# Experts of a gated MoE kernel: all eight chunks of gate and up split, the output copied by one engine, one signal per chunk of w_down

## The reference

```python
a = jnp.einsum('td,edf->tef', hf, w_gate[g])
b = jnp.einsum('td,edf->tef', hf, w_up[g])
act = (jax.nn.silu(a) * b) * cg[..., None]
y = y + jnp.einsum('tef,efd->td', act, w_down[g])
```

## Time and profile before

| | |
|---|---|
| Runs (us) | 947.41, 949.59, 951.21; median 949.59 |
| Profiled execution (us) | 948.92 |
| Its span, first to last instruction (us) | 946.9 |
| TensorE busy | 920.6 us, 97% |
| VectorE busy | 698.5 us, 74% |
| ScalarE busy | 442.0 us, 47% |
| GpSimd busy | 83.3 us, 9% |
| Moved by DMA | 170.13 MB, mean 180 GB/s |

### The profile page before, as it was taken

The page is one execution under the profiler, slowest core; times in us unless marked ns, Lnnn a source line. Parts: engine busy times, 40 slices in busy tenths (PEclk is TensorE's granted clock), DMA queues, the critical chain, the costliest instruction groups (busy, mean ns, idle before and its releaser), DMA issues.

```text
span 946.9 us, 13479 instructions
## 1 busy us (share of the span) xinstructions
PE 920.6 (97%) x5016; PEld 815.8 (86%) x5016; DVE 698.5 (74%) x951; ACT 442.0 (47%) x694; POOL 83.3 (9%) x109
## 2 busy tenths in 40 slices
PE   8999999999999999999999999999999999999984
PEld 7999999999999999999888888778777878787751
DVE  5648797777878877437721348798989898989847
ACT  6612221312111138822401324587878787878714
POOL 0000000010000000000000002322121212121100
PEclk9999999999999999999999999999999999999998
DMA  9020111111111211012511765599999999999559
GB/s 301 12 67 23 45 46 45 39 37 45 56 35 46 89 45 45 12 34 90 174 57 37 259 244 222 195 348 396 365 381 376 362 370 359 378 376 380 226 205 367
DMA packets 73801, 170.13 MB, mean 180 GB/s; under 512 B 10907, under 2 KB 48299, under 8 KB 60401
## 3 DMA queue, kind: packets, MB, share of 16 engines
q1 hardware_dynamic: 64529, 152.05, 44.8%
q0 software_dynamic: 9216, 17.32, 5.7%
HBM read 156.83 MB, written 22.47 MB: 189 GB/s over the span
## 4 chain that ended last, share of the span: by engine, by line
PE 90%; DVE 5%; ACT 3%; issue 1%; DMA 1%; SPq 0%; ACTq 0%; DVEq 0%
PE ps L1682 42%; PE ps L1963 16%; PE ps L1870 11%; PE ps L1941 10%; PE ps L1956 3%; PE ps L1919 2%; PE ps L1824 2%; PE ps L1705 1%; DVE x L1656 1%; PE ps L1992 1%; PE ps L1811 1%; DVE x L1642 1%; PE ps L1927 1%; DVE hT L1083 1%; DMA xs<-in_x_prompt 1%
## 5 line engine op out<-in xcount | busy, mean ns | idle before, releaser
L1682 PE MATMUL ps<-hT,w_hi 128*128 128x352 f32 x1344 | 329.5, 326 | 0.8 <-DVE hT L1083 0.8
L1682 PEld LDWEIGHTS ps<-hT,w_hi 128*128 128x128 f32 x1344 | 235.9, 189 | 2.0 <-DVE hT L1083 1.2
L1682 PE MATMUL ps<-hT,w_lo 128*128 128x352 f32 x672 | 218.3, 325 | 0.0
L1157 DVE SCALAR_TENSOR_TENSOR C<-V,w_dw,C 128x1086 f32<-128x1086 f32 x120 | 154.8, 1345 | 0.3
L1531 DVE TENSOR_TENSOR wgu_lo<-wgu,wgu_hi 128x1024 fp32r<-128x1024 f32 (+1 forms) x128 | 133.8, 1086 | 1.3 <-ACT wgu_hi L988 1.1
L1682 PEld LDWEIGHTS ps<-hT,w_lo 128*128 128x128 f32 x672 | 126.2, 188 | 0.0
L988 ACT ACTIVATE wgu_hi<-wgu 128x1024 fp32r<-128x1024 f32 x124 | 114.9, 956 | 6.5 <-PE ps L1963 5.3
L1963 PE MATMUL ps<-wgu_hi,XT_hi 128*128 128x512 f32 x224 | 100.0, 447 | 0.0
L1558 DVE TENSOR_TENSOR wdn_lo<-wdn,wdn_hi 128x1024 fp32r<-128x1024 f32 x62 | 73.2, 1223 | 27.3 <-ACT wdn_hi L1024 27.3
L1090 DVE TENSOR_TENSOR w_lo<-w_raw,w_hi 128x1024 fp32r<-128x1024 f32 (+1 forms) x44 | 45.2, 1028 | 64.2 <-ACT w_hi L791 64.2
L1870 PE MATMUL ps<-wo_hi,hT 128*128 128x512 f32 x288 | 91.6, 399 | 0.0
(11 more groups left out here) (258 smaller groups left out, 1491.7 us busy)
## 6 DMA issues: line engine op xcount, KB each, us to landing
wgu<-in_w_gate SPq DMA_DIRECT2D x32, 1024.0 KB, 9.1
wgu<-in_w_up SPq DMA_DIRECT2D x32, 1024.0 KB, 11.5
wdn<-in_w_down SPq DMA_DIRECT2D x32, 1024.0 KB, 13.4
w_raw<-in_w_in SPq DMA_DIRECT2D x28, 512.0 KB, 3.8
yy<-YK SPq DMA_DIRECT2D x8, 1024.0 KB, 11.7
xs<-in_x_prompt SPq DMA_DIRECT2D x8, 512.0 KB, 7.6
wo_raw<-in_w_out SPq DMA_DIRECT2D x8, 512.0 KB, 4.9
xr<-in_x_prompt SPq DMA_DIRECT2D x16, 256.0 KB, 2.7
```

Of the source, the lines that this page charges most:

```text
L1157: op = dve.scalar_tensor_tensor(out=C[:, g, :], in0=V[:, g, k:k + CWID], scalar=w_dw[:, g, k:k + 1], in1=C[:, g, :], op0=ALU.mult, op1=ALU ...
L1682: op = pe.matmul(ps[:, bank_of(m, c), 0:CH], a[s][:, k, :], r[:, k, c * CH:(c + 1) * CH], start=(k == 0 and q == 0), stop=(k == K - 1 and ...
```

## The change

`WHOLE` becomes 0, so all eight chunks of gate and up are split, in four pieces of two chunks, and the tile `XT`, its copy and its fp32 product are gone. Both halves of `Y` are copied by ScalarE, one after the other; VectorE only makes the index column, which no longer waits for the down product. ScalarE gives a signal for each of the two chunks of w_down, and VectorE waits for each by itself, where it waited for both.

```diff
--- before.py
+++ after.py
@@ -44,7 +44,7 @@
 PASSES = (T + CAP - 1) // CAP
 TOP = 2048.0
 WB = 4
-WHOLE = 1
+WHOLE = 0
 PIECES = [slice(c, min(c + 2, KD)) for c in range(WHOLE, KD, 2)]
 PAIRS = len(PIECES)
 AHEAD = 2
@@ -228,7 +228,6 @@
         wdn = [at(f"wdn{u}", [P, KF, D], F32, w_off[u] + 16384) for u in range(WB)]
         X = at("X", [P, 4, D], F32, r_h + 49152)
         Y = [at(f"Y{u}", [P, D], F32, o) for u, o in enumerate((r_uv + 24576, r_uv + 28672, r_s + 4352, r_wo))]
-        XT = at("XT", [P, WHOLE, P], F32, r_yp + 24576)
         XT_hi = at("XT_hi", [P, KD - WHOLE, P], F32R, r_yp + 24576 + WHOLE * P * 4)
         XT_lo = at("XT_lo", [P, KD - WHOLE, P], F32R, r_yp + 24576 + KD * P * 4)
         assert 24576 + (2 * KD - WHOLE) * P * 4 <= 32768
@@ -528,7 +527,7 @@
 
         BIAS, LN_G, LN_B, SCALE = 0, GR, 2 * GR, 3 * GR
 
-        PREP = 10
+        PREP = 9
         RANK_BANK = (7, 3)
         FIND_BANK, FIND_AGAIN = 2, 4
 
@@ -1004,7 +1003,6 @@
 
                 act.wait_ge(s_tx, it + 1)
                 wait(act, s_gp, it * PAIRS)
-                act.activation(XT[:, :, 0:CAP], ps[:, 0, :].rearrange("p (c t) -> p c t", c=4)[:, 0:WHOLE, 0:CAP], ACT.Copy)
                 act.activation(XT_hi[:, :, 0:CAP], split_chunks(), ACT.Copy).then_inc(s_xtA, 1)
 
             def at_hi(u, it):
@@ -1016,13 +1014,14 @@
 
                 act.wait_ge(s_down, it + 1)
                 wait(act, s_ys[u], 16 * uses)
-                act.activation(Y[u][0:CAP, 0:512], ps[0:CAP, 4 + 2 * (u % 2), :], ACT.Copy).then_inc(s_yA, 1)
+                for h in range(2):
+                    op = act.activation(Y[u][0:CAP, h * 512:(h + 1) * 512], ps[0:CAP, 4 + 2 * (u % 2) + h, :], ACT.Copy)
+                op.then_inc(s_yA, 1)
 
             def down_hi(p, i, u, halves):
                 act.wait_ge(s_wn[u], 16 * (p * (GE // WB) + i + 1))
                 for c in range(KF):
-                    op = act.activation(halves[c][:], wdn[u][:, c, :], ACT.Copy)
-                op.then_inc(s_dnhi, 1)
+                    act.activation(halves[c][:], wdn[u][:, c, :], ACT.Copy).then_inc(s_dnhi, 1)
 
             def step(p, i, u):
                 it = p * GE + i * WB + u
@@ -1545,16 +1544,14 @@
 
                 dve.tensor_copy(g_now[0:CAP, u:u + 1], column(g_idx, e)).then_inc(s_gc, 1)
 
-            def y_out(it, u, uses, e):
-                dve.wait_ge(s_down, it + 1)
+            def s_column(u, uses, e):
                 wait(dve, s_ys[u], 16 * uses)
 
-                dve.tensor_copy(s_now[0:CAP, u:u + 1], column(s_idx, e))
-                dve.tensor_copy(Y[u][0:CAP, 512:1024], ps[0:CAP, 5 + 2 * (u % 2), :]).then_inc(s_yD, 1)
+                dve.tensor_copy(s_now[0:CAP, u:u + 1], column(s_idx, e)).then_inc(s_yD, 1)
 
             def down_lo(it, u, halves):
-                dve.wait_ge(s_dnhi, it + 1)
                 for c in range(KF):
+                    dve.wait_ge(s_dnhi, it * KF + c + 1)
                     op = dve.tensor_tensor(wdn_lo[u][:, c, :], wdn[u][:, c, :], halves[c][:].bitcast(F32), ALU.subtract)
                 op.then_inc(s_dnlo, 1)
 
@@ -1575,7 +1572,7 @@
                     for j in range(AHEAD, PAIRS):
                         gate_lo(it + 1, nu, j)
                 if not (isinstance(i, int) and i == 0 and u == 0):
-                    y_out(it - 1, (u - 1) % WB, p * (GE // WB) + i + (u - 1) // WB, i * WB + u - 1)
+                    s_column((u - 1) % WB, p * (GE // WB) + i + (u - 1) // WB, i * WB + u - 1)
                 dve.wait_ge(s_athi, it + 1)
                 dve.tensor_tensor(AT_lo[:, :, 0:CAP], act_turned(u), AT_hi[:, :, 0:CAP].bitcast(F32),
                                   ALU.subtract).then_inc(s_act, 1)
@@ -1612,7 +1609,7 @@
                 prep(dve.tensor_scalar(rank[:], rank[:], -float(CAP), None, ALU.add))
                 if isinstance(p, int):
                     dve.wait_ge(s_cnt, 1)
-                for half in (XT[:], XT_hi[:].bitcast(F32), XT_lo[:].bitcast(F32)):
+                for half in (XT_hi[:].bitcast(F32), XT_lo[:].bitcast(F32)):
                     prep(dve.memset(half[:, :, CAP:P], 0.0))
                 if isinstance(p, int):
                     dve.wait_ge(s_h2st[0], 16 * ((TILES + 1) // 2))
@@ -1626,7 +1623,7 @@
                 for j in range(AHEAD):
                     gate_lo(p * GE + 1, 1, j)
                 groups(dve, step, p)
-                y_out(p * GE + GE - 1, WB - 1, (p + 1) * (GE // WB) - 1, GE - 1)
+                s_column(WB - 1, (p + 1) * (GE // WB) - 1, GE - 1)
 
             rounds(dve, one)
 
@@ -1931,7 +1928,6 @@
                 b = u % 2
                 pe.wait_ge(s_act, it + 1)
                 wait(pe, s_yA, it - 1)
-                wait(pe, s_yD, it - 1)
                 pe.wait_ge(s_dnlo, it + 1)
                 for h in range(2):
                     cols = slice(h * 512, (h + 1) * 512)
@@ -1952,8 +1948,6 @@
                 pe.wait_ge(s_xtA, it + 1)
                 wait(pe, s_act, it - 1)
                 pe.wait_ge(s_wl[u], 32 * (p * (GE // WB) + i + 1))
-                for c in range(WHOLE):
-                    pe.matmul(both, XT[:, c, :], wgu[u][:, :, c, :], start=(c == 0), stop=False)
                 pe.wait_ge(s_xtD, it + 1)
                 for j in range(PAIRS):
                     pe.wait_ge(s_gl, it * PAIRS + j + 1)
```

## The result

| | before | after |
|---|---|---|
| median of 12 runs (us) | 948.51 | 954.34 |
| lowest to highest | 946.75 to 951.21 | 952.87 to 955.87 |
| ratio, 95% interval | | 1.0064 [1.0054, 1.0074] |
| profiled execution, its span | 948.92, 946.9 | 955.87, 954.1 |

The change made the kernel slower by 0.64%, 6.1 us (the medians differ by 5.8). The forecast was 948.9, no difference that can be measured, with a range that ended at 952.5.

A forecast was written before the change was run, and what follows sets the result against it. TensorE was taken to set the pace, with loads having no spare time. Start +1.1, saving -5.4 and end +0.85 gave -3.45; late loads cut this to -0.7, so 948.9 us in terms of the median, range 944.5 to 952.5.

The forecast's parts named there:

- TensorE's own saving: In each loop step, three fp32r matmuls replace the fp32 chunk: 0.18 us saved, a step of 9.26, -5.4 us over 30 steps.
- ScalarE, VectorE and the signals at nothing: In each loop step, the added work of ScalarE and VectorE and the changed signals cost nothing, covered by TensorE's work.
- Rival 3: At each step's first matmul, XT_lo becomes the bound: +13.8 us, with start and end +15.8, or 965.4; chance 0.05.
- The start: In the first two steps, three more matmuls follow the wait for XT_lo: 0.7 to 1.4 us, taken as +1.1.
- The loads take back the rest: Late in the loop, loads landing no earlier leave 1.6 us of a 3.9 us lead; net with the end -0.7.
- the wait for loads that I expected after 830 us: Late in the loop, ScalarE's wgu_hi waits for a load, up to 3 us at a time, TensorE idle by less.
- The prediction's own sign of being wrong: In the loop, the prediction counts as wrong if loads stall it by more than its whole lead, taken as 3.9 us.
- The end: In the last step, AT_hi comes 0.50 us later and the last Y about 0.35 later, together +0.85.
- Rival 2: Over the whole loop, loads pin the pace and leave no lead: +0.85 to +2, about 951 us; chance 0.13.
- rival 1: Over the whole loop, loads keep pace and land earlier with their issue: -3.45, or 946.1 us; chance 0.2.

The follow-up runs named there:

- e2_copy_signals: Against the kernel before: ScalarE alone copies Y and each w_down chunk has its signal, the fp32 chunk stays; 949.55 us, ratio 1.0005.
- e3_keep_running: The changed kernel plus identity matmuls in TensorE's idle time before the first products of steps 0 and 1; 952.16 us, ratio 1.0029.
- c2_after_light_keep: The changed kernel with w_down loads of 8 columns instead of 1,024, plus identity matmuls before the first products of steps 0 and 1; 946.23 us, ratio 0.9972.
- e4_hi_first: The changed kernel with the first piece's four products that need only XT_hi run before the two that need XT_lo; 948.55 us, ratio 0.9996.
- c1_hi_first_end: e4_hi_first with, in the last step, AT_hi made before Y is copied and the last Y copied by ScalarE and VectorE; 947.99 us, ratio 0.9992.
- c3_split_hi_first: Against the kernel before: only the split of all eight chunks, with the product order of e4_hi_first; 948.78 us, ratio 1.0006.
- e1_split_only: Against the kernel before: only the split of all eight chunks, Y copied by both engines and one w_down signal as before; 953.12 us, ratio 1.0040.

## Why the prediction was wrong

**TensorE's own saving** was right. From one step's products to the next it is 9.25 and 9.28 us (they start at 641.91, 651.16 and 660.44), against the forecast 9.26.

**ScalarE, VectorE and the signals at nothing** was right. TensorE is busy throughout from 647.6 to 818.1, and e2_copy_signals pays for the end alone. Rival 3, XT_lo as the bound of each step, did not come.

**The start** is the step that failed. "The first fp32r matmul waits for the same XT_lo, and three more matmuls come behind it": the first half held in step 0, with 601.87 where I wrote about 601.6; in step 1 it was 612.16, for about 610.0. But I priced what comes behind it by 0.23 us a product, the price at the full clock, and bounded the whole at 1.4 us. Measured, the loss is 5.06 by the end of step 1. The fp32 chunk not only filled the time of XT_lo; by running then it kept TensorE's clock up. Without it 24 products took 7.34 and 7.35 us, not 5.56, which is 3.6 for two steps; e3_keep_running and c2_after_light_keep give 3.1 and 3.6 for it. The remaining 1.5 is the wait of steps 0 and 1 and the three added products; e3_keep_running, at the full clock, has 1.95 for it. My upper bound of 1.4 was little under that. It is the fall of the clock that was priced at nothing: I took a TensorE that waits for a TensorE that costs only its wait. Nothing in the trace of before shows a clock below 1.00 in this stretch. But it has a price of this kind at the end of the loop, which I did not read. There TensorE is idle for 2.03 us; the granted clock is 0.73 from 908 to 910 and 0.50 from 910 to 912, and eight products take 5.40 us that take 3.43 soon after (chain of waits):

```profile
906.03 2.03 issue
908.05 5.40 PE ps L1992 x8
...
916.47 3.43 PE ps L1992 x8
```

The Trainium skill, in "TensorE: Matmul & The Clock Gate", section "What's actually happening", says that TensorE's default state is throttled and that activity releases it. These traces agree: 0.51 after 2.22 us of idle time in the changed kernel, 1.00 once e3_keep_running fills it.

**The loads take back the rest** was right as a mechanism and too small in size. I let the landings move back by at most the 1.1 us of the start. The start was late by 5.06, the first two up weights issued within the loop left 2.6 and 5.1 us later, and the landing of the weight issued near 796 moved back by 9.9. The rates account for most of that: by 647.6 the loads are behind by 40 GB/s x 47.6 us, 1.9 MB or 5.1 us at 376 GB/s; the 6 GB/s less in the next two stretches of 56.8 and 56.9 us add 1.8. The other 3.0 I can't place. So the wait for loads that I expected after 830 us, "with TensorE idle by less", came at 825.7, and TensorE's wait there cost 2.27 - 1.25 = 1.0 us at first and 5.65 - 2.27 = 3.4 in the next step, of which 7.32 - 5.56 = 1.8 is the third fall of the clock. The prediction's own sign of being wrong, loads that stall the loop by more than its whole lead, came true: TensorE was stalled by 4.4 us, and it had no lead but was 1.25 late.

**The end** was right in its two terms: AT_hi 0.47 later after Y (forecast 0.50), the last scatter 0.33 later after the last Y's start (0.35). But behind the last scatter, where the forecast put nothing, this execution lost another 2.05 us, and that stays open.

**The rivals.** Rival 2, loads that pin the loop at about 951, was nearest in time. With the start at its right price it gives 948.9 + (5.06 - 1.1) + 1.6 = 954.5, where 1.6 is the lead that the forecast still left to TensorE; the median is 954.34. That they agree so closely is luck: the sum starts from 949.59, the median of three runs, where that of twelve is 948.51, and it leaves out the 2.05 us behind the last scatter. Nor was the whole loop pinned: up to 815 TensorE made up 3.8 us, and only then did the loads hold it. With the cover back (e4_hi_first, c1_hi_first_end) the time is where the forecast had it, at no difference from before, and rival 1, loads that keep pace, is excluded by their waits of 13.1 and 14.7 us.

## What to carry to other kernels

Before a product is removed, see what the engine would do in its time: here the product that filled a wait on TensorE also kept its clock up, and the clock cost as much (3.6 us) as leaving the product out saved in 20 steps (20 x 0.18). Look for the price of such a fall in the whole trace of before, not only in the stretch that the change touches. The same cover could be had by order alone, by running first the products whose operands were ready (e4_hi_first). And where the DMA share is already 1.02, price lateness at the start as a debt that the loads did not make up here, and compare with a light load before working on the engines.

## What was not expected of the hardware

Idle times of 2.22 and 1.53 us on TensorE were each followed by the lower clock, at 1.8 us for the 24 products behind them; idle times of 1.06 us (kernel before), 1.00 and 1.00 us (e4_hi_first, c1_hi_first_end) at the same place were not. The length of one idle time does not decide it: late in the loop of c3_split_hi_first 1.91 us was not followed by a fall, with 5.72 us for the 24 products (timeline, then chain of waits), nor was 1.69 us in c1_hi_first_end, while in e4_hi_first 1.15 and 0.32 us were. Of the seven traces in which TensorE waits late in the loop, two show a fall there (the changed kernel and e4_hi_first).

```profile
824.57 0.49 PE L1925 MATMUL ps<-ident,act_out 104*128 104x104 f32 x2 [1.91 <-DVE act_out L1569]
```

```profile
825.34 5.72 PE ps L1962 x24
```

GpSimd's indirect DMA instructions take longer in the changed kernel: from 600 to 910 us the scatter takes 1848 ns on average and the gather 1798, where the kernel before has 1047 and 1143 (groups of instructions in that stretch):

```profile
L756 POOL DMA_INDIRECT YK<-Y,s_now x31 | 57.3, 1848 | 182.6 <-DVE s_now L1550 182.6
L746 POOL DMA_INDIRECT X<-H,g_now x29 | 52.1, 1798 | 17.1 <-DVE g_now L1545 8.6 <-issue 8.5
```

e1_split_only has it too (GpSimd busy for 21.99 us from 648 to 704, the kernel before 12.82, the changed kernel 23.74) and e2_copy_signals does not (13.36), so it comes with the split. The loop of e4_hi_first, with instructions as long, loses nothing by them. The cause is open.
